# Attention of a hybrid decoder layer: twelve turned chunks per head packed into ten, a third PSUM bank for turning, pair work moved between engines

## The chip, the cores and the metric

One core of one Trainium2 chip runs the whole layer in one launch. The metric is the device time of the launch in microseconds; the kernel before takes 707.17 us in the median of three runs (706.26 to 708.14).

## The reference

Batch 1, 1024 positions, width 1024, all in float32. The layer is a conditioned mixer with two groups of heads that share one input projection:

```python
h = rmsnorm(x, norm_in) * (1.0 + scale) + shift          # shift, scale, gate = silu(c) @ w_ada + b_ada
(cb, cc, cu, cz, aq, ak, av, az, iq, ik, iw) = split(h @ w_in)
y_conv = group_rmsnorm(short_conv_mixer(cb, cc, cu), gn_conv, 8) * silu(cz)
# per query: 8 indexer heads give a score of every key, the 256 best causal keys are kept
score = sum_h iw_h * relu(dot(iq_h, ik) * idx_scale);  sel = top_k(score, 256)
p = softmax(where(selected and causal, q k^T * HEAD_DIM**-0.5, -inf))   # 8 heads of 64
y_attn = group_rmsnorm(p @ v, gn_attn, 8) * silu(az)
out = rmsnorm(x + gate * (concat(y_conv, y_attn) @ w_out), norm_f)   # as the kernel applies it
```

The group norm of the attention divides each head's output by its own root mean square, so the softmax's denominator need not be divided out: it only scales the epsilon. The kernel uses that.

## The kernel before

Every matrix product is made of fp32r products of split operands: a tile X is split into a rounded high part XH (a copy on ScalarE, ACT) and the rest XL (a subtraction on VectorE, DVE, or GpSimd, POOL), and a product is XH·WH + XL·WH + XH·WL. TensorE (PE) therefore does three matmuls where one would do.

The program is written out by hand, one in-order queue for each engine, tied by counting semaphores. It has four stretches: the load and norm of x and the modulation (0 to about 60 us); 37 units of the input projection, between whose matmuls the indexer, the top-k search (on DVE) and the convolution lie (to about 482 us); the attention (482 to 621 us); and the output projection with the last norm (to the end).

The modulation's weights arrive in pieces (`wa`): eight of 512 KB for part 0, and four and four tiles of two 256 KB DMAs for parts 1 and 2. `ada_sum` (L1376 and on) waits with `wa_sem` for its piece, then multiplies and adds on DVE. Each piece of parts 0 and 1 has a semaphore of its own; pairs of pieces of part 2 share one.

The attention handles 8 heads one after the other. For head h the work is:

- `logits(u)`, u = 8h + i: PE makes the logits of query block i (128 queries) against keys 0 to 128(i+1), two matmuls for each 512 columns, into PSUM banks 2-3 (u even) or 0-1 (u odd). `row_max(u)` on DVE adds the mask in place and takes the maximum, `weights(u)` on ACT makes exp into `prob` in SBUF and sums it.
- Turning and values: for each half sb of the queries (blocks 0 to 3, and 4 to 7) and each key block j, a chunk k. `turn(k)` on PE transposes up to four 128x128 tiles of `prob` into a PSUM bank, 4 + k % 2; `split_prob(k)` on ACT copies it out as the high part phH; `low_prob(k)` on DVE subtracts to get phL; `values(k)` on PE multiplies both by V into bank 6 + sb. A head has 12 chunks (STEPS), of 512, 384, 256 and 128 columns in the first half and five of 512, then 384, 256, 128 in the second. `turn(k)` waits for `low_prob(k - 2)`, `values` runs PV_LAG = 2 chunks behind, phH has 3 buffers and phL 2.
- `other_half` (ACT) and `head_out` (DVE) add the two halves of the product and put them in `ya`.

The logits, maxima and exponentials of head h+1 lie between the chunks of head h, at half steps x = 2k, 2k+1 given by the tables LOGITS_AT, MAX_AT and EXP_AT. After every second head there is the work of a pair t (heads 2t, 2t+1) of 128 rows: `square_den` and `keep_den` (DVE) with `denominators` (PE); `pair_square` (POOL, two halves), `group_sums` (PE, one fp32 matmul for each half into banks 3 and 1), `pair_gate` (DVE, 1024 columns) and `pair_add` (DVE, two halves, out of PSUM). For the first three pairs this lies in head 2t+2, so heads 2, 4 and 6 (counted from 0) carry pair work. In heads 2 to 5 ACT and POOL also split one tile of w_out each (`out_high`, `out_low`). In the last head there are no logits to make; 16 steps of the output projection (`out_step`, EARLY_PARTS) lie between the chunks, and ACT and DVE split yconv and w_out. After it `pair_log`, `pair_root` and `pair_scale` finish the attention's gate and norm, and PE goes through the rest of the output projection.

Lines: `turn` L778, `logits` L808 and L809, `values` L890 and L891, `group_sums` L908, `out_step` L939 to L941, `weights` L1142, `split_prob` L1151, `other_half` L1216, `out_high` L1241, `ada_sum` L1378 and L1381, `row_max` L1589, `low_prob` L1597, `head_out` L1605, `pair_gate` L1627, `pair_add` L1636, `pair_scale` L1644, `low_out` L1649, `pair_square` L1818, `out_low` L1823.

## Time and profile before

| what | value |
|---|---|
| median of 3 runs | 707.17 us |
| the profiled execution, its own time | 706.91 us |
| its span, first to last instruction | 704.9 us |
| PE busy | 662.3 us, 94% |
| PE weight loads busy | 546.2 us, 77% |
| DVE busy | 460.4 us, 65% |
| ACT busy | 375.4 us, 53% |
| POOL busy | 207.4 us, 29% |
| mean granted clock of TensorE | 0.997 |

A matmul's busy time is modelled and includes its way through the array, so consecutive matmuls overlap and a PE that is called 90% busy can have more room than 10%. The shares are means over the whole span; the attention has its own, which the rows below show.

### The profile page before, as it was taken

How to read it: one execution, taken by the hardware profiler on the slowest of the kernel's cores; microseconds unless marked ns; L12 is line 12 of the kernel's file. 1: busy time of each engine (PE TensorE's matmuls, PEld its weight loads, DVE VectorE, ACT ScalarE, POOL GpSimd, SP SyncE). 2: the span in 40 equal slices, each digit the busy share in tenths (PEclk: the TensorE clock that was granted, in tenths of full speed). 3: DMA queues.
4: the chain of work that ended last, by engine and by line, in shares of the span. 5: the costliest groups of instructions: out<-in, count | busy, mean ns of one | idle time of the engine just before them, and what ended most of it. 6: DMA issues, size and time to landing. Idle time of an engine off the chain costs nothing.

```text
span 704.9 us, 8934 instructions
## 1 busy us (share of the span) xinstructions
PE 662.3 (94%) x3203; PEld 546.2 (77%) x3203; DVE 460.4 (65%) x777; ACT 375.4 (53%) x558; POOL 207.4 (29%) x105
## 2 busy tenths in 40 slices
PE   0899999899999999999999999999999988999996
PEld 0889977788888888888888887887767666788884
DVE  5894535567889999992079530016898989577635
ACT  5866345556651324453454624636878787784202
POOL 1001223433224334746755667410011110100000
PEclk9999999999999999999999999999999999999999
DMA  8950597533223111111100731085944340221431
GB/s 322 378 203 1 146 156 172 162 96 91 90 89 120 38 53 36 55 60 31 60 32 31 248 110 60 1 179 131 289 120 121 89 121 1 60 91 71 168 120 60
DMA packets 27910, 78.63 MB, mean 112 GB/s; under 512 B 3986, under 2 KB 8410, under 8 KB 27868
## 3 DMA queue, kind: packets, MB, share of 16 engines
q1 hardware_dynamic: 27524, 77.03, 36.8%
q10 hardware_dynamic: 344, 1.05, 0.6%
q8 instruction: 25, 0.41, 0.3%
q14 instruction: 17, 0.14, 0.1%
HBM read 61.25 MB, written 13.41 MB: 106 GB/s over the span
## 4 chain that ended last, share of the span: by engine, by line
PE 72%; DVE 8%; issue 7%; DMA 5%; ACT 4%; SPq 2%; POOL 1%; ACTq 1%; DVEq 0%; POOLq 0%
PE ps L755 15%; PE ps L756 15%; PE ps L757 15%; PE ps L939 4%; PE ps L940 4%; PE ps L941 4%; PE ps L778 3%; DVE acc L1381 2%; DMA raw<-in_w_units 2%; PE ps L828 2%; PE ps L827 2%; PE ps L808 2%; PE ps L809 2%; DMA xin<-in_x 1%; DVE phL L1597 1%
## 5 line engine op out<-in xcount | busy, mean ns | idle before, releaser
L755 PE MATMUL ps<-hH,wH 128*128 128x512 f32 (+1 forms) x544 | 211.8, 389 | 2.0 <-issue 1.9
L757 PE MATMUL ps<-hH,wL 128*128 128x512 f32 (+1 forms) x544 | 210.1, 386 | 0.0
L756 PE MATMUL ps<-hL,wH 128*128 128x512 f32 (+1 forms) x544 | 210.1, 386 | 0.0
L1749 POOL TENSOR_TENSOR wL<-raw,wH 128x1024 fp32r<-128x1024 f32 x35 | 85.4, 2440 | 187.7 <-ACT wH L993 179.5
L755 PEld LDWEIGHTS ps<-hH,wH 128*128 128x128 f32 x544 | 102.2, 188 | 22.5 <-issue 4.0
L757 PEld LDWEIGHTS ps<-hH,wL 128*128 128x128 f32 x544 | 102.1, 188 | 20.4
L756 PEld LDWEIGHTS ps<-hL,wH 128*128 128x128 f32 x544 | 102.2, 188 | 18.3
L1589 DVE CUSTOM_DVE_ANT_0 ps<-ps,bias 128x128 f32<-128x128 f32 (+3 forms) x64 | 48.7, 761 | 45.7 <-PE ps L809 43.7
L1597 DVE TENSOR_TENSOR phL<-ps,phH 128x512 fp32r<-128x512 f32 (+1 forms) x96 | 52.6, 554 | 16.9 <-ACT phH L1151 15.3
L1193 ACT ACTIVATE relu<-ps,wabs 128x384 f32<-128x384 f32 (+5 forms) x48 | 40.1, 849 | 38.1 <-PE ps L828 18.6
L1483 DVE SCALAR_TENSOR_TENSOR score<-relu,wsgn,score 128x384 f32<-128x384 f32 (+5 forms) x42 | 49.7, 1184 | 15.2 <-ACT relu L1193 12.2
L1504 DVE TENSOR_SCALAR_CACHE_REDUCE above<-score,srch 128x384 bf16<-128x384 f32 (+5 forms) x60 | 56.8, 946 | 2.1
L1151 ACT ACTIVATE phH<-ps 128x512 fp32r<-128x512 f32 (+1 forms) x96 | 46.1, 490 | 18.1 <-PE ps L778 16.8
L778 PE MATMUL ps<-identF,prob 128*128 128x128 f32 x288 | 49.1, 280 | 6.8 <-DVE phL L1597 3.6
L1142 ACT ACTIVATE prob<-ps,nmx 128x128 f32<-128x128 f32 (+3 forms) x64 | 47.4, 741 | 15.1 <-DVE nmx L1589 15.1
L778 PEld LDWEIGHTS ps<-identF,prob 128*128 128x128 f32 x288 | 34.5, 141 | 22.9 <-DVE phL L1597 13.1
L940 PE MATMUL ps<-hL,yH 128*128 128x512 f32 x128 | 50.3, 393 | 0.0
L1818 POOL TENSOR_TENSOR ysq<-ya 128x512 f32<-128x512 f32 x8 | 9.9, 1234 | 134.3 <-DVE ya L1605 134.3
L993 ACT ACTIVATE wH<-raw 128x1024 fp32r<-128x1024 f32 x37 | 38.8, 1052 | 10.6 <-DMA raw<-in_w_units 8.3
L890 PE MATMUL ps<-phH,VV 128*128 128x512 f32 (+1 forms) x96 | 38.5, 402 | 0.0
L808 PE MATMUL ps<-ks,qs 128*128 128x512 f32 (+2 forms) x96 | 35.3, 368 | 3.4 <-ACT prob L1142 2.1
L891 PE MATMUL ps<-phL,VV 128*128 128x512 f32 (+1 forms) x96 | 33.1, 346 | 0.0
(225 smaller groups left out, 1129.4 us busy)
## 6 DMA issues: line engine op xcount, KB each, us to landing
raw<-in_w_units SPq DMA_DIRECT2D x36, 512.0 KB, 3.3
ks<-qk_halves SPq DMA_DIRECT2D x32, 256.0 KB, 5.8
xin<-in_x SPq DMA_DIRECT2D x8, 512.0 KB, 7.4
wa<-in_w_ada SPq DMA_DIRECT2D x8, 512.0 KB, 11.8
wa<-in_w_ada SPq DMA_DIRECT2D x16, 256.0 KB, 8.0
gw<-in_w_ada SPq DMA_DIRECT2D x8, 512.0 KB, 4.1
qs<-qk_halves SPq DMA_DIRECT2D x16, 256.0 KB, 4.0
wo<-in_w_out SPq DMA_DIRECT2D x8, 512.0 KB, 9.4
```

The lines of the kernel that those rows point to most:

```text
L755: pe.matmul(out, wH[slot(n)][:, kt, :], hH[:, kt, cols], start=(kt == 0), stop=False)
L756: pe.matmul(out, wH[slot(n)][:, kt, :], hL[:, kt, cols], start=False, stop=False)
L757: mm = pe.matmul(out, wL[slot(n)][:, kt, :], hH[:, kt, cols], start=False, stop=(kt == KT - 1))
L778: mm = pe.transpose(ps[:, 4 + k % 2, P * b:P * b + P], prob_of(sb, b)[:, P * j:P * j + P], identF[:])
L808: pe.matmul(dst[:, o:e], q, ks1[h % 2][:, o:e], start=True, stop=False)
L940: pe.matmul(out, yH[b % 4][:, ct, :], hL[:, ct, cols], start=False, stop=False)
L1142: A(prob_of(sb, i % 4), logit_bank(u), ACT.Exp, bias=nmx[:, u:u + 1], scale=-1.0, accum_out=den[:, h // 2, h % 2, i:i + 1]).then_inc(s_exp, 1)
L1483: v.scalar_tensor_tensor(score_of(i), relu[:, u % 2, 0:n], wsgn[:, i, h:h + 1], score_of(i), ALU.mult, ALU.add).then_inc(s_score, 1)
L1504: v.tensor_scalar(above[:, 0:(i + 1) * P], score_of(i), cand[:, b:b + 1], None, ALU.is_ge, ALU.add, accum_out=count[:, b:b + 1]).then_inc( ...
L1589: v.tensor_tensor_reduce(src, src, bias_of(i), -ATT_SCALE, 3.0e38, ALU.add, ALU.min, nmx[:, u:u + 1]).then_inc(s_mx, 1)
L1597: v.tensor_tensor(phL[:, k % 2, P * c:HALF], ps[:, 4 + k % 2, P * c:HALF], phH[:, k % NPH, P * c:HALF].bitcast(F32), ALU.subtract).then_in ...
L1749: g.tensor_tensor(wL[slot(n)][:], raw[slot(n)][:], wH[slot(n)][:].bitcast(F32), ALU.subtract).then_inc(s_wL, 1)
```

## The change

A head has ten chunks in place of twelve. CHUNKS lists the key blocks of each: blocks 1 and 3 of the first half share a bank (384 and 128 columns), as do blocks 5 and 7 of the second. A packed bank is split by one instruction of 512 columns on ACT and one on DVE; `turn` and `values` handle the two blocks one after the other. The transposes and the matmuls stay the same in number and width.

Turning uses three banks in rotation: 4, 5, and a third that is borrowed, the upper half of a logits pair (3, or 0 in the last head) or the first half's output bank (6), by the step in the head. `turn(k)` waits for `low_prob(k - 3)`, and for the borrowed bank to be free; `values` runs three chunks behind, phH has 4 buffers and phL 3. To make room in SBUF `ysq` has one buffer in place of two. The tables of the half steps are new.

For the first three pairs, `pair_gate` and `pair_add` go from DVE to POOL, each in two halves. POOL does not read the sums in PSUM, so ACT copies each half out first (`keep_sums`). The group sums of both halves use bank 1. The multiplication by gn_attn goes from the gate to `pair_scale`, which becomes a scalar_tensor_tensor. The last pair stays on DVE.

Of the modulation's weights, pieces 0 and 1 of part 0 share a semaphore, as do 2 and 3, and of part 1 pieces 0 and 1, and 2 and 3 (WA_SHARES). A wait on such a semaphore is for both pieces. New semaphores are s_ygP, s_addP and s_sums.

```diff
+WA_SHARES = ((0, 0, 1, 1, 2, 3, 4, 5), (0, 0, 1, 1), (0, 0, 1, 1))
...
-NPH = 3
-PV_LAG = 2
-STEPS = 12
-LOGITS_AT = (4, 11, 13, 16, 18, 21, 23, 26)
-MAX_AT = (6, 11, 14, 16, 17, 22, 23, 25)
-EXP_AT = (10, 14, 17, 17, 22, 24, 27, 30)
+NPH = 4
+NPL = 3
+PV_LAG = 3
+CHUNKS = ([(0,)] + [(1, 3)] + [(2,)], [(j,) for j in range(5)] + [(5, 7)] + [(6,)])
+STEPS = len(CHUNKS[0]) + len(CHUNKS[1])
+LOGITS_AT = (2, 5, 10, 13, 15, 16, 18, 20)
+MAX_AT = (1, 5, 9, 12, 14, 15, 17, 20)
...
-TMP_AT, OUT_AT = 4, 5
+TMP_AT, OUT_AT = 5, 5
+THIRD_IN_OUT = (7, 8, 9, 0, 1)
...
-SUMS_AT = {24 * (2 * t + 2) + 11 + 4 * half: (t, half) for t in range(NT - 1) for half in range(2)}
-SUMS_AT[LAST + 17] = (NT - 1, 0)
-GATE_AT = {24 * (2 * t + 2) + 12: t for t in range(NT - 1)}
-ADD_AT = {24 * (2 * t + 2) + 13 + 4 * half: (t, half) for t in range(NT - 1) for half in range(2)}
-ADD_AT[LAST + 16] = (NT - 1, 0)
...
+HEAD = 2 * STEPS
...
+SUMS_AT = {HEAD * (2 * t + 2) + 5 + 8 * half: (t, half) for t in range(NT - 1) for half in range(2)}
+SUMS_AT[LAST + 15] = (NT - 1, 0)
+KEEP_SUMS_AT = {HEAD * (2 * t + 2) + 6 + 8 * half: (t, half) for t in range(NT - 1) for half in range(2)}
+OUT_HIGH_AT = {HEAD * (2 + ct) + 13: ct for ct in range(4)}
+OUT_HIGH_AT.update({LAST + x: 4 + n for n, x in enumerate((11, 14, 17, 18))})
+OUT_LOW_AT = {LAST + x: 4 + n for n, x in enumerate((13, 18, 19))}
+EARLY_PARTS = {3: 2, 4: 2, 5: 2, 6: 2, 7: 3, 8: 3, 9: 2}
...
                 [at(f"prob1_{b}", [P, (b + 5) * P], F32, kb) for b, kb in enumerate((186, 65.5, 68.5, 72))]]
         phH = at("phH", [P, NPH, HALF], F32R, 80)
-        phL = at("phL", [P, 2, HALF], F32R, 88)
+        phL = [at(f"phL{i}", [P, HALF], F32R, kb) for i, kb in enumerate((88, 90, 78))]
...
         woB = [at(f"woB{i}", [P, 2, D], F32R, kb) for i, kb in enumerate((145, 113))]
-        ysq = [at(f"ysq{i}", [P, HALF], F32, kb) for i, kb in enumerate((86, 205))]
+        ysq = at("ysq", [P, HALF], F32, 205)
...
+        CH = [(h, sb, js) for h in range(NH) for sb in range(2) for js in CHUNKS[sb]]
+        CH_AT = {(h, sb, j): n for n, (h, sb, js) in enumerate(CH) for j in js}
...
+        def all_up_to(h, sb, j):
+            return max(CH_AT[(h, sb, x)] for x in range(j + 1))
         def last_chunk(g):
-            return CH_AT[(g // 2, g % 2, 4 * (g % 2) + 3)]
+            return all_up_to(g // 2, g % 2, 4 * (g % 2) + 3)
...
+            return range(max(0, j - 4 * sb), 4)
+        def place(js, sb, j):
+            return -P * blocks_of(sb, j).start if js.index(j) else 0
+        def width(k):
+            h, sb, js = CH[k]
+            return slice(0 if len(js) > 1 else P * blocks_of(sb, js[0]).start, HALF)
...
-            return (1, 7)[half]
+            return 7 if t == NT - 1 and half else 1
+        def turn_bank(k):
+            h, at_step = k // STEPS, k % STEPS
+            if k % 3 < 2:
+                return 4 + k % 3
+            if at_step in THIRD_IN_OUT:
+                return 6
+            return 3 if h < NH - 1 else 0
+        def turned_into(bank, h, steps):
+            ks = [STEPS * h + x for x in steps if turn_bank(STEPS * h + x) == bank]
+            return ks[-1] + 1 if ks else 0
...
-            return s_wa[g][i // 2] if g == 2 else s_wa[g][i]
+            return s_wa[g][WA_SHARES[g][i]]
...
-                h, sb, j, c = CH[k]
-                if j == 0:
+                h, sb, js = CH[k]
+                bank, at_step = turn_bank(k), k % STEPS
+                if js[0] == 0:
                     pe.wait_ge(s_exp, NB * h + 4 * sb + 4 if k else 6)
-                if k >= 2:
-                    pe.wait_ge(s_pl, k - 1)
-                for b in range(c, 4):
-                    mm = pe.transpose(ps[:, 4 + k % 2, P * b:P * b + P], prob_of(sb, b)[:, P * j:P * j + P], identF[:])
+                if k >= 3:
+                    pe.wait_ge(s_pl, k - 2)
+                if bank == 6:
+                    pe.wait_ge(s_o, 2 * h + 1 if at_step > 5 else 2 * h - 1)
+                elif bank == 3:
+                    pe.wait_ge(s_exp, NB * h + (7 if h else 8))
+                elif bank == 0:
+                    pe.wait_ge(s_exp, NB * NH)
+                for j in js:
+                    for b in blocks_of(sb, j):
+                        o = P * b + place(js, sb, j)
+                        mm = pe.transpose(ps[:, bank, o:o + P], prob_of(sb, b)[:, P * j:P * j + P], identF[:])
                 mm.then_inc(s_tp, 1)
...
+                if h >= 3 and h % 2 == 1 and i == 5:
+                    pe.wait_ge(s_sums, h - 1)
+                if h and i == 4:
+                    pe.wait_ge(s_pl, turned_into(3, h - 1, range(2, 7)))
...
-                h, sb, j, c = CH[k]
+                h, sb, js = CH[k]
...
-                if j == 0 and g >= 2:
+                if js[0] == 0 and g >= 2:
                     pe.wait_ge(s_o, g - 1)
-                out = ps[:, 6 + sb, P * c:HALF]
-                pe.matmul(out, VV[:, j, h, :], phH[:, k % NPH, P * c:HALF], start=(j == 0), stop=False, skip_group_check=True)
-                pe.matmul(out, VV[:, j, h, :], phL[:, k % 2, P * c:HALF], start=False, stop=(j == 4 * sb + 3),
-                          skip_group_check=True).then_inc(s_pv, 1)
+                if k % STEPS == 0 and turned_into(6, h, (0, 1)):
+                    pe.wait_ge(s_pl, turned_into(6, h, (0, 1)))
+                for j in js:
+                    cols = slice(P * blocks_of(sb, j).start, HALF)
+                    src = slice(cols.start + place(js, sb, j), cols.stop + place(js, sb, j))
+                    out = ps[:, 6 + sb, cols]
+                    pe.matmul(out, VV[:, j, h, :], phH[:, k % NPH, src], start=(j == 0), stop=False, skip_group_check=True)
+                    mm = pe.matmul(out, VV[:, j, h, :], phL[k % NPL][:, src], start=False, stop=(k == last_chunk(g)),
+                                   skip_group_check=True)
+                mm.then_inc(s_pv, 1)
...
-                    pe.wait_ge(s_exp, NB * (2 * t + 2) + 7 + half)
+                    pe.wait_ge(s_exp, NB * (2 * t + 2) + 8)
+                    if half:
+                        pe.wait_ge(s_sums, 2 * t + 1)
...
-                pe.matmul(ps[:, sums_bank(t, half), :], pairs[:], ysq[half][:], start=True, stop=True).then_inc(s_yss, 1)
+                pe.matmul(ps[:, sums_bank(t, half), :], pairs[:], ysq[:], start=True, stop=True).then_inc(s_yss, 1)
...
+                        pe.wait_ge(s_pl, turned_into(0, NH - 1, range(2, 7)))
                         if half:
-                            pe.wait_ge(s_add, 2 * NT - 1)
+                            pe.wait_ge(s_add, 1)
...
+            def keep_sums(t, half):
+                act.wait_ge(s_yss, 2 * t + half + 1)
+                act.wait_ge(s_ygP, 2 * t + half + 1)
+                A(pair_cols(t, half), ps[:, sums_bank(t, half), :], ACT.Copy).then_inc(s_sums, 1)
             def pair_log(t, half=None):
-                act.wait_ge(s_add, 2 * t + (half if half is not None else 1) + 1)
+                if t < NT - 1:
+                    act.wait_ge(s_addP, 2 * t + 2)
+                else:
+                    act.wait_ge(s_add, half + 1)
                 z = pair_cols(t, half)
...
-                dve.wait_ge(wa_sem(g, i), 16 * each * (2 if g == 2 else 1))
+                dve.wait_ge(wa_sem(g, i), 16 * each * WA_SHARES[g].count(WA_SHARES[g][i]))
...
-                if k >= 2:
-                    dve.wait_ge(s_pv, k - 1)
-                v.tensor_tensor(phL[:, k % 2, P * c:HALF], ps[:, 4 + k % 2, P * c:HALF],
-                                phH[:, k % NPH, P * c:HALF].bitcast(F32), ALU.subtract).then_inc(s_pl, 1)
+                if k >= NPL:
+                    dve.wait_ge(s_pv, k - NPL + 1)
+                v.tensor_tensor(phL[k % NPL][:, width(k)], ps[:, turn_bank(k), width(k)],
+                                phH[:, k % NPH, width(k)].bitcast(F32), ALU.subtract).then_inc(s_pl, 1)
...
+            def pair_scale(t):
+                dve.wait_ge(s_yrs, t + 1)
+                dve.wait_ge(s_ygP, 2 * t + 2)
+                v.scalar_tensor_tensor(ya[:, t, :], ya[:, t, :], vec[:, V_GA + t:V_GA + t + 1], azs[:, t, :],
+                                       ALU.mult, ALU.mult).then_inc(s_ya, 1)
...
+                if t or half:
+                    pool.wait_ge(s_yss, 2 * t + half)
                 z = ya[:, t, HALF * half:HALF * half + HALF]
-                g.tensor_tensor(ysq[half][:], z, z, ALU.mult).then_inc(s_ysq, 1)
...
+            def pair_gate(t, half):
+                pool.wait_ge(s_ysq, 2 * t + half + 1)
+                cols = slice(HALF * half, HALF * half + HALF)
+                g.tensor_tensor(ya[:, t, cols], ya[:, t, cols], azs[:, t, cols], ALU.mult).then_inc(s_ygP, 1)
+            def pair_add(t, half):
+                pool.wait_ge(s_sums, 2 * t + half + 1)
+                pool.wait_ge(s_din, 32 * (t + 1))
+                cols = slice(HALF * half, HALF * half + HALF)
+                g.tensor_tensor(azs[:, t, cols], azs[:, t, cols], dden[:, cols], ALU.add).then_inc(s_addP, 1)
+            for t in range(NT - 1):
+                pair_square(t, 0)
+                pair_gate(t, 0)
+                if t:
+                    out_low(2 * t - 1)
+                pair_square(t, 1)
+                pair_gate(t, 1)
+                pair_add(t, 0)
+                pair_add(t, 1)
+                if t < 2:
+                    out_low(2 * t)
             pair_square(NT - 1, 0)
```

## Rows read from the trace of the kernel before

**Rows 1.** PE's busy time: stretch, length, busy (count), clock, DMA share, GB/s

```profile
100.00:420.00 320.00, 316.12 (x1429) 1.00 0.30 90
...
660.00:705.00 45.00, 38.20 (x169) 0.98 0.26 94
```

**Rows 2.** Busy time by head: stretch, length, PE, PEld, DVE, ACT, POOL, clock, DMA

```profile
514.27:531.46 17.19, 15.91 (x90) 11.88 (x88) 15.65 (x34) 13.50 (x32) 3.45 (x2) 1.00 0.41 95
531.46:547.19 15.73, 14.09 (x87) 11.33 (x85) 13.77 (x33) 13.37 (x32) 3.38 (x2) 1.00 0.54 136
...
580.08:598.00 17.92, 16.59 (x92) 12.18 (x90) 16.40 (x34) 13.27 (x33) 1.04 (x1) 1.00 0.01 1
...
598.80:620.88 22.08, 21.20 (x100) 16.61 (x101) 13.46 (x22) 18.46 (x27) 2.08 (x1) 0.92 0.16 49
```

**Rows 3.** Groups by form, DVE, 514.27 to 547.19: busy us, mean ns, idle before

```profile
L1597 DVE TENSOR_TENSOR phL<-ps,phH 128x512 fp32r<-128x512 f32 x12 | 8.2, 687 | 2.2 <-ACT phH L1151 1.9
L1589 DVE CUSTOM_DVE_ANT_0 ps<-ps,bias 128x1024 f32<-128x1024 f32 x3 | 3.7, 1233 | 0.3
...
L1597 DVE TENSOR_TENSOR phL<-ps,phH 128x384 fp32r<-128x384 f32 x4 | 2.2, 552 | 0.0
...
L1636 DVE TENSOR_TENSOR azs<-ps,dden 128x512 f32<-128x512 f32 x2 | 1.4, 680 | 0.0
L1627 DVE SCALAR_TENSOR_TENSOR ya<-ya,vec,azs 128x1024 f32<-128x1024 f32 x1 | 1.3, 1280 | 0.0
...
L1597 DVE TENSOR_TENSOR phL<-ps,phH 128x128 fp32r<-128x128 f32 x4 | 1.1, 287 | 0.0
```

**Rows 4.** Groups by form, ACT, the same stretch

```profile
L1151 ACT ACTIVATE phH<-ps 128x512 fp32r<-128x512 f32 x12 | 7.1, 596 | 2.5 <-PE ps L778 2.5
...
L1216 ACT ACTIVATE tmp<-ps 64x512 f32<-64x512 f32 x4 | 2.4, 592 | 0.1
L1142 ACT ACTIVATE prob<-ps,nmx 128x1024 f32<-128x1024 f32 x2 | 2.2, 1110 | 0.0
...
L1151 ACT ACTIVATE phH<-ps 128x384 fp32r<-128x384 f32 x4 | 1.9, 487 | 0.0
...
L1151 ACT ACTIVATE phH<-ps 128x128 fp32r<-128x128 f32 x4 | 1.1, 278 | 0.9 <-PE ps L778 0.8
```

**Rows 5.** Waits, same stretch: who for whom, us in total, times, longest

```profile
PE ps L778 <- ACT prob L1142: 0.6, 2, 0.3
...
ACT phH L1151 <- PE ps L778: 3.4, 9, 0.8
...
DVE phL L1597 <- ACT phH L1151: 1.9, 4, 0.9
```

**Rows 6.** Order of time: start us, us, instruction [idle before]; POOL and DVE

```profile
549.96 1.04 POOL L1818 TENSOR_TENSOR ysq<-ya 128x512 f32<-128x512 f32 x1 [7.54 <-DVE ya L1605]
...
610.62 2.08 POOL L1818 TENSOR_TENSOR ysq<-ya 128x512 f32<-128x512 f32 x1 [26.72 <-DVE ya L1605]
...
610.57 1.23 DVE L1649 TENSOR_TENSOR hL<-wo,woB 128x1024 fp32r<-128x1024 f32 x1
```

**Rows 7.** Order of time, ACT and DVE, 534 to 536 us

```profile
534.69 0.60 ACT L1151 ACTIVATE phH<-ps 128x512 fp32r<-128x512 f32 x1 [0.58 <-PE ps L778]
...
535.32 0.69 DVE L1597 TENSOR_TENSOR phL<-ps,phH 128x512 fp32r<-128x512 f32 x1 [0.89 <-ACT phH L1151]
```

**Rows 8.** DVE's sums of part 0, and the issues of pieces 2 and 3

```profile
21.43 8.24 DVE L1381 SCALAR_TENSOR_TENSOR acc<-wa,small,acc 128x1024 f32<-128x1024 f32 x6
...
L524 SPq DMA_DIRECT2D wa<-in_w_ada x2: 480/1245/2010, 7.8 to 8.3; - x2
DMA to landing us min/median/max: 12.6/13.0/13.4
```

**Rows 9.** The last head: PE's time and granted clock in one microsecond; order of time

```profile
602.00:603.00 1.00, 1.00 (x4) 0.50 0.01 4
...
601.26 0.77 PE L939 MATMUL ps<-hH,yH 128*128 128x512 f32 x1 [0.45 <-issue]
```

More of the change, by code:

```diff
@@ L1145, in split_prob @@
             def split_prob(k):
-                h, sb, j, c = CH[k]
                 act.wait_ge(s_tp, k + 1)
@@ L1262, in _ @@
                         other_half(TMPS[x])
+                    if x in KEEP_SUMS_AT:
+                        keep_sums(*KEEP_SUMS_AT[x])
                     if x in OUT_HIGH_AT:
@@ L1694, in _ @@
                 low_y(b, 1)
-            pair_scale(NT - 1, 1)
+            last_scale(1)
             dve.wait_ge(s_gate, 16)
```

112 lines of the change are left out of this document (45 added, 67 removed).

## The prediction

> **What bounds the kernel now.** I read the whole kernel first by stretches, then the attention head by head. In the middle of the projection PE is busy 316.12 of 320 us [rows 1]; nothing in the change touches PE's work there, so it stays. Of the 45 us from 660 on PE is busy for the first 38.2, to its last matmul at 698.2 [rows 1], and what follows is the last block's norm; that stays too. So only the attention can move, and what it gains or loses moves the end one for one, as long as PE then has the output projection's operands in time.
>
> In the attention the windows by head [rows 2] show two kinds of head. Head 3 (1 and 5 are the same within 0.02) lasts 15.73 us with DVE 13.77, ACT 13.37 and PE 14.09 busy; heads 2 and 6 (4 is as 2), which carry the pair work, last 17.19 and 17.92 with DVE 15.65 and 16.40 busy, ACT still 13.5 and 13.3. DVE grows by 1.88 from one kind to the other and the head by 1.46. PE's number is modelled, and the head follows DVE, not PE, so I take DVE as the nearest limit, ACT next, and PE as the one that waits. No engine is full, however: in a light head DVE has 1.96 us idle. The largest piece is one wait of 0.89 at the head's start [rows 7]: ACT has ended the last exponential and stands 0.58 us until PE has turned the next chunk, and DVE, behind ACT, starts only at 535.32. With two banks PE can't turn that chunk ahead. Over two heads ACT waits 3.4 us in nine places for turns, DVE 1.9 for splits [rows 5]. So a head costs DVE's work plus about 10% in round trips over the two banks.
>
> **Packing.** Per head two chunks go. On DVE a 384 and a 128 instruction (552 + 287 ns) become one of 512 (687): 0.15 us by durations, twice, 0.30 [rows 3]; busy times overlap a little back to back, so I take 0.2. On ACT 487 + 278 - 596 = 0.17, twice, 0.34 [rows 4]; I take 0.3. On PE two waits go and no work.
>
> **Pair work, heads 2, 4, 6.** DVE loses one gate of 1.28 and two adds of 0.68, 2.64 us by durations [rows 3]; the difference of DVE's busy time between the two kinds of head (1.88, where the light ones have about 0.45 of denominator work instead) says 2.3 to 2.4, which I take. ACT gains two copies of 512 columns out of PSUM at the 0.59 of the tmp copy [rows 4]: +1.2. The trace doesn't show a wait for `keep_sums`: it stands early in the head behind the last exponential, PE's sum and the gate on POOL. Behind it in ACT's queue are the next split and so DVE's next chunk. I bound its wait by 0 and by 0.9 (the longest of DVE's waits [rows 5]) and take 0.3. POOL gains two gates and two adds at 1.04 each [rows 6], 4.2 us a pair, beside the 3.4 that it does in a head now [rows 2]: some 11 us in the 33 us of two heads. Its half 1 chain (square and gate, 2.1 us after `head_out` at half step 5) has until half step 14, four and a half chunks, some 6 us: hidden. If each ran at the 2.08 of the disturbed square it would still take 4.2.
>
> This last case is one for the Trainium skill. At 610.62 POOL's square took 2.08 us in place of 1.04 while DVE ran a subtraction with both inputs in SBUF, itself not slowed (1.23) [rows 6]. The page "GPSIMD Engine Reference", section "Specifications", says that POOL shares its SBUF interfaces with DVE and contends with DVE instructions that have two SBUF inputs, and its section on engine selection gives elementwise work to VectorE; it speaks against the move. By its rule the price falls where DVE's inputs are both in SBUF; here `low_prob`, `head_out` and `row_max` all read PSUM, and the sum stays.
>
> **The new limits.** Light head: DVE 13.77 - 0.2 = 13.6, ACT 13.37 - 0.3 = 13.1. Pair head: DVE 15.65 - 0.2 - 2.35 = 13.1, ACT 13.5 - 0.3 + 1.2 = 14.4. So the limit of the pair heads moves from DVE to ACT.
>
> **Three banks, lag 3.** A chunk's round trip is a turn (some 0.6, by the 0.58 that ACT stood for one [rows 7]), a split of 0.60 and a subtraction of 0.69, with the handing over some 2.1 us. Over two banks that is 1.05 us a chunk at best, over three 0.7, where the queues need 1.36 to 1.5 a chunk. So a turn can nearly always be made ahead, and most of DVE's 1.96 us of idle time in a light head should go, of which the waits for splits, 0.95 a head by the mean of two, are the half. Not all: the first chunk of a head's second half still needs the eighth exponential (the PE wait of 0.3, twice, in [rows 5]), logits for a new head need the seventh, and a borrowed bank has waits of its own: bank 3 on that same seventh exponential, which lies one step ahead on ACT, and bank 6 on `head_out`, also a step ahead. I bound the gain from this between 0 and 1.4 in a head (1.96 less what 33 hand-overs of some 20 ns cost). For a light head I take 0.9, the size of the wait that the extra bank answers to [rows 7]; with the 0.2 of DVE the head goes from 15.73 to 14.6, a gain of 1.1. For a pair head: 14.4 of ACT work, 0.3 for `keep_sums`, and the 0.9 to 1.0 us that a head still loses at its start and in handing over, 15.7; from 17.19 that is 1.5.
>
> **The last head.** It lasts 22.08 us, ACT busy 18.5, PE 21.2. Its mean granted clock is 0.92: for about 3.5 us around 602 it was 0.50, the lower level (1.2 GHz), and 8% of the head, 1.8 us, were lost [rows 2, 9]; at 601.26 PE had just stood 0.45 us. If PE waits less there, the fall may not come: a gain of 1.8. Against that, ten steps leave less time: PE's group sum at half step 15 needs POOL's square after `head_out` at half step 11, and the second half of block 1 needs the add; PE could stand 1 us. Range of the term -2.2 to +1.0; I take -0.7.
>
> The page "TensorE: Matmul & The Clock Gate" of the Trainium skill, section "A second HAM failure mode: psum-queue depth-cycling", says that a PE that idles a little between groups as banks cycle can swing between the clocks. By that the term would be near -2.
>
> **Weights' semaphores.** DVE makes seven sums of part 0, the last six from 21.43 to 29.67 without a gap, 1.39 us apart [rows 8]; the sum of piece 2, at 22.83, now also needs piece 3. That was issued at 8.3 and landed 13.4 later, at 21.7: 1.1 us of cover. Piece 1, issued ahead of piece 2 in one queue, should be in ahead of it, and piece 2 is by 20.4 (7.8 and 12.6), before the second sum. Cost nothing; without the cover, each microsecond of lateness of piece 3 costs one, since these sums lie on the chain. Part 1's sums come 8 us after part 0's, and its DMAs follow on in the same queue; nothing. **`pair_scale`** becomes a form that took 1.28 us as the gate [rows 3] in place of one of some 1.2, three times, 0.2 us after the attention, behind it PE has 48 matmuls of blocks 2 and 3 queued: nothing. One `ysq` buffer: the square of half 1 comes later than the sum of half 0 in any case: nothing.
>
> **The sum.** Heads 0, 1, 3, 5: 4 x 1.1 = 4.4. Heads 2, 4, 6: 3 x 1.5 = 4.5. Last head 0.7. Together 9.6, from the profiled execution's own 706.91 (its span of 704.9 and 2.0 around it): 697.3 us. The median of the runs is 0.26 above that execution, within their spread, so I leave it.
>
> **Rivals.**
> (a) The banks give all: every named wait goes, light heads at 14.2 (1.5 saved), pair heads at ACT's 14.4 plus 0.4 (2.4), last head 2.0. 6.0 + 7.2 + 2.0 = 15.2, 691.7 us. For it: a turn can be three chunks ahead, and the waits are of the kind that this removes. Against: each queue stays in order and the two exponentials at the head's border are still in series.
> (b) The waits only change their names: the tables' order, not the banks, makes them. Then light heads gain the 0.3 of packing and pair heads 0.7 (DVE's relief less ACT's load). 1.2 + 2.1 = 3.3, 703.6 us. For it: DVE waited only four times in two heads for a split.
> (c) Slower: the eighth exponential. `turn` of the second half waits for it on PE, and behind it there are the values and the logits of the next head. Before, it had its place after the third split of a head, now after the second; its own chain is a maximum of 1.23 and an exponential of 1.11 [rows 3, 4], with their logits and reads of the sums some 3.6 us. If it comes later than the three steps give, some 4.1 us, PE, then ACT and DVE stand. It decides from 1.3 us of extra wait a head: by then light heads (4 x 1.1) and pair heads (3 x 1.5) have nothing left; at 2.0 light heads lose 0.9 and pair heads 0.5 each and the last head gains nothing: 3.6 + 1.5 = 5.1, 712.0 us. Against: the maximum of that block is already behind turn 0 and the chain fits by half a microsecond.
>
> **How the numbers follow.** Forecast 0.57, (a) 0.22, (b) 0.13, (c) 0.08. About 0.3% (2.1 us) is what a measurement of this kernel can tell from no change. Faster by more than that means under 705.0: all of the forecast and of (a), most of (b), 0.87 together, cut to 0.85 for what the unknown wait of `keep_sums` could add. Same 0.07, slower 0.08. The range: at the bottom into (a), 690; at the top (b) with a little more, 704.5.
>
> **What would show it.** Light heads near 14.6 us and pair heads near 15.7 in the windows; DVE's wait for splits at a head's start under 0.3; DVE about 13.1 busy in a pair head and ACT 14.4, ACT now first; POOL's gates and adds at about 1.04. The start of PE's projection unchanged, at the same microsecond. The clock in the last head tells its term. Wrong it would be if PE's waits for exponentials grow past a microsecond a head, if ACT stands before the copy of the sums, or if the heads stay at their length while the idle time moves from DVE to another.

## The result, and the profile after

The changed kernel takes 698.49 us (median of six runs, 696.65 to 699.95), the kernel before 706.71 beside it; the ratio is 0.9881, 95% interval 0.9857 to 0.9906. The forecast was 697.3. The profiled execution took 698.44 us with a span of 696.6: 8.3 less than before.

The attention again head by head, now from the start of one head's last exponential (1024 columns) to the start of the next. Cut in this way heads 0 to 6 of before last 16.77, 15.72, 17.18, 15.73, 17.18, 15.72 and 17.18 us. The windows of the kernel after; columns: stretch, length, PE busy (count), PEld, DVE, ACT, POOL, granted clock, DMA share, GB/s; the answer to [rows 2]:

```profile
483.44:499.83 16.39, 14.85 (x83) 12.72 (x83) 12.22 (x28) 12.76 (x29) 0.00 (x0) 0.90 0.92 299
499.83:514.31 14.48, 13.68 (x87) 11.52 (x86) 13.37 (x31) 12.32 (x29) 2.33 (x2) 1.00 0.79 212
514.31:529.86 15.55, 15.16 (x90) 12.15 (x89) 12.93 (x29) 14.24 (x32) 7.21 (x5) 1.00 0.45 102
529.86:543.97 14.11, 13.69 (x87) 11.64 (x86) 13.29 (x31) 13.16 (x30) 4.68 (x3) 1.00 0.60 151
543.97:559.48 15.51, 15.14 (x90) 12.26 (x89) 12.88 (x29) 14.25 (x32) 7.23 (x5) 1.00 0.43 103
559.48:574.55 15.07, 13.75 (x87) 11.54 (x86) 13.38 (x31) 13.16 (x30) 4.67 (x3) 1.00 0.57 138
574.55:590.07 15.52, 15.08 (x93) 12.36 (x91) 12.94 (x29) 13.41 (x31) 4.86 (x4) 1.00 0.01 2
```

Read down the lengths first. The seven heads gave 8.85 us. The three light heads 1, 3 and 5 gained 1.24, 1.62 and 0.65, though the same work is done in each; the pair heads gained 1.63, 1.67 and 1.66. In a pair head DVE fell from 15.65 to 12.9 and ACT rose from 13.5 to 14.2. In head 3 PE is busy 13.69 of 14.11 us, where before it was 14.09 of 15.73.

The groups by form of DVE and then ACT over heads 2 and 3 (columns as in [rows 3, 4], to which they answer), and below them POOL in order of time in head 2 (start, us, instruction, idle before), against [rows 6]:

```profile
L1653 DVE TENSOR_TENSOR phL<-ps,phH 128x512 fp32r<-128x512 f32 x17 | 11.7, 687 | 1.1 <-ACT phH L1197 1.1
L1653 DVE TENSOR_TENSOR phL<-ps,phH 128x256 fp32r<-128x256 f32 x4 | 1.7, 422 | 0.4 <-ACT phH L1197 0.3
...
L1197 ACT ACTIVATE phH<-ps 128x512 fp32r<-128x512 f32 x17 | 10.2, 597 | 1.5 <-PE ps L814 1.4
...
L1272 ACT ACTIVATE azs<-ps 128x512 f32<-128x512 f32 x2 | 1.2, 600 | 0.1
```

```profile
517.44 1.04 POOL L1880 TENSOR_TENSOR ysq<-ya 128x512 f32<-128x512 f32 x1 [8.77 <-DVE ya L1661]
518.56 1.28 POOL L1891 TENSOR_TENSOR ya<-ya,azs 128x512 f32<-128x512 f32 x1
519.80 1.30 POOL L1898 TENSOR_TENSOR azs<-azs,dden 128x512 f32<-128x512 f32 x1
523.86 1.29 POOL L1898 TENSOR_TENSOR azs<-azs,dden 128x512 f32<-128x512 f32 x1 [2.76 <-ACT azs L1272]
```

The durations on DVE and ACT are those of before. POOL's gate and add take 1.28 to 1.30 us each, not the 1.04 of its square, but POOL stood 2.76 us before one of them, so it has room. ACT hardly stands before `keep_sums` (0.1).

Over the same two heads the waits, against [rows 5], columns: who for whom, us in total, times, longest:

```profile
DVE ps L1646 <- PE ps L847: 1.9, 3, 1.1
...
ACT phH L1197 <- PE ps L814: 1.4, 6, 0.2
DVE phL L1653 <- ACT phH L1197: 1.4, 4, 0.7
...
PE ps L846 <- ACT prob L1189: 0.4, 1, 0.4
PE ps L846 <- DVE phL L1653: 0.4, 1, 0.4
```

ACT's waits for turns fell from 3.4 us to 1.4, and no single one is above 0.2. DVE now waits for logits instead, that is, for PE: 1.9 us where it was 0.5. What is left of PE's own waits is 0.8 in two heads.

Outside these heads two things moved, and together they give back 0.62. DVE's sums of the weights are not one of them: they still follow one another in 1.39 us without a gap, so the shared semaphores cost nothing, as [rows 8] had it:

```profile
22.45 8.24 DVE L1438 SCALAR_TENSOR_TENSOR acc<-wa,small,acc 128x1024 f32<-128x1024 f32 x6
```

(They begin 1.02 us later than before, but so does DVE's whole queue: its first square of x starts at 13.45 instead of 12.47, when x has landed.) The attention starts 0.37 us later than before. In the kernels whose edits touch nothing ahead of it this start varies from 482.6 to 484.1, and is 484.9 to 485.3 in E7, E9 and E11, in whose profiles the granted clock fell once near 130 us; so I read nothing into it. And from the last head's exponential to the end of PE's last matmul it is 99.90 us after 99.65: nothing gained, which hides terms of opposite sign (below, with the step "last head").

### The profile page after: what moved, and what is told of

It reads as the page before. It is cut to its first block, busy times and chain, and to the rows that moved or that the text cites. A ratio compares the mean times of both kernels' runs of the same rounds, so it can differ in the third digit from the quotient of the medians.

```text
span 696.6 us, 8911 instructions
## 1 busy us (share of the span) xinstructions
PE 658.8 (95%) x3203; PEld 548.5 (79%) x3203; DVE 450.7 (65%) x752; ACT 376.7 (54%) x548; POOL 222.3 (32%) x117
## 3 DMA queue, kind: packets, MB, share of 16 engines
q10 hardware_dynamic: 344, 1.05, 0.6%
## 4 chain that ended last, share of the span: by engine, by line
PE 77%; DVE 7%; DMA 5%; ACT 4%; issue 3%; SPq 2%; POOL 1%; ACTq 1%; DVEq 0%
PE ps L782 15%; PE ps L783 15%; PE ps L784 15%; PE ps L986 4%; PE ps L987 4%; PE ps L988 4%; PE ps L814 3%; PE ps L846 3%; DVE acc L1438 2%; PE ps L847 2%; DMA raw<-in_w_units 2%; PE ps L866 2%; PE ps L865 2%; PE ps L934 2%; PE ps L933 2%
## 5 line engine op out<-in xcount | busy, mean ns | idle before, releaser
L1653 DVE TENSOR_TENSOR phL<-ps,phH 128x512 fp32r<-128x512 f32 (+1 forms) x80 | 50.5, 634 | 14.4 <-ACT phH L1197 11.3
L1197 ACT ACTIVATE phH<-ps 128x512 fp32r<-128x512 f32 (+1 forms) x80 | 44.1, 552 | 9.1 <-PE ps L814 8.6
L814 PE MATMUL ps<-identF,prob 128*128 128x128 f32 x288 | 45.7, 278 | 1.1 <-ACT prob L1189 0.8
L933 PE MATMUL ps<-phH,VV 128*128 128x512 f32 (+1 forms) x96 | 36.8, 384 | 0.0
```

The costliest lines, as they stand in the source:

```text
L814: mm = pe.transpose(ps[:, bank, o:o + P], prob_of(sb, b)[:, P * j:P * j + P], identF[:])
L933: pe.matmul(out, VV[:, j, h, :], phH[:, k % NPH, src], start=(j == 0), stop=False, skip_group_check=True)
L1653: v.tensor_tensor(phL[k % NPL][:, width(k)], ps[:, turn_bank(k), width(k)], phH[:, k % NPH, width(k)].bitcast(F32), ALU.subtract).then_inc ...
```

## The experiments

The length of a head is the measure that tells most here: the total also carries the start and short falls of the granted clock, which come at other places from one execution to the next. The table has every kernel's seven heads, from its one profiled execution, and its time; "before" for each call lay between 706.7 and 707.7. Head 0 holds a fall of the clock in the kernel after, E2, E4 and E7, heads 1, 3 and 5 each hold one in E5, and none of the other heads in the table does.

| kernel | head 0 | 1 | 2 | 3 | 4 | 5 | 6 | median us | ratio to before (interval) |
|---|---|---|---|---|---|---|---|---|---|
| before | 16.77 | 15.72 | 17.18 | 15.73 | 17.18 | 15.72 | 17.18 | 706.71 | |
| after | 16.39 | 14.48 | 15.55 | 14.11 | 15.51 | 15.07 | 15.52 | 698.49 | 0.9881 (0.9857-0.9906) |
| E1 two banks | 15.27 | 14.52 | 15.77 | 14.53 | 16.01 | 14.51 | 15.77 | 699.54 | 0.9898 (0.9873-0.9922) |
| E2 pair work on DVE | 16.40 | 14.48 | 17.24 | 14.11 | 16.60 | 15.05 | 16.60 | 702.57 | 0.9928 (0.9906-0.9950) |
| E3 both | 15.29 | 14.52 | 17.00 | 14.52 | 16.99 | 14.51 | 17.05 | 703.64 | 0.9952 (0.9934-0.9970) |
| E4 step 6 in the out bank | 16.41 | 14.50 | 17.43 | 14.13 | 15.52 | 15.83 | 15.53 | 700.91 | 0.9924 (0.9895-0.9953) |
| E5 before, lag 3 | 18.35 | 18.54 | 18.93 | 18.56 | 18.92 | 18.55 | 18.18 | 720.49 | 1.0195 (1.0173-1.0218) |
| E6 after, PE loaded | 15.73 | 15.16 | 16.46 | 14.86 | 16.44 | 15.78 | 16.46 | 705.73 | 0.9986 (0.9955-1.0017) |
| E7 after, DVE loaded | 16.61 | 14.86 | 16.13 | 14.87 | 15.52 | 15.81 | 15.52 | 702.65 | 0.9935 (0.9915-0.9956) |
| E8 after, ACT loaded | 15.09 | 14.73 | 15.76 | 14.55 | 15.72 | 15.30 | 15.55 | 700.61 | 0.9902 (0.9878-0.9927) |
| E9 E3 with lag 2 | 15.60 | 14.67 | 17.23 | 14.68 | 17.23 | 14.68 | 17.26 | 705.62 | 0.9973 (0.9956-0.9989) |
| E10 before, PE loaded | 17.40 | 16.34 | 17.83 | 16.35 | 17.82 | 16.33 | 17.82 | 712.86 | 1.0068 (1.0042-1.0095) |
| E11 before, DVE loaded | 17.77 | 16.77 | 17.99 | 16.77 | 17.99 | 16.78 | 18.00 | 712.38 | 1.0068 (1.0043-1.0093) |
| E12 bank at fixed steps | 14.81 | 14.12 | 15.51 | 14.11 | 15.51 | 14.10 | 15.54 | 696.47 | 0.9855 (0.9826-0.9884) |

**E1: the changed kernel with two banks.**

```diff
-            if k % 3 < 2:
-                return 4 + k % 3
-            if at_step in THIRD_IN_OUT:
-                return 6
-            return 3 if h < NH - 1 else 0
+            return 4 + k % 2
...
-                if k >= 3: pe.wait_ge(s_pl, k - 2)
+                if k >= 2: pe.wait_ge(s_pl, k - 1)
```

> The kernel after with turning over banks 4 and 5 only (turn k waits for the subtraction of k-2); packing, lag 3, tables, pair work on POOL stay. Theory A (round trips over two banks were the main cost, the third bank removed them): heads without pair work go from 14.1-14.5 back to about 15.4 us, pair heads from 15.5 to about 16.8, in all +8 us, about 706. Rival B (the relief of DVE by packing and by moving the pair work did it, the third bank is beside the point): under 0.3 us a head, in all under +2 us, about 700.

Heads 1 to 6 sum to 91.11 us against 90.24 with three banks. (All seven sum to 106.38 against 106.63, but head 0 of the kernel after has a fall of the clock in it.) Heads 2, 3, 4 and 6 are 0.22 to 0.50 longer without the third bank, but head 5 is 0.56 shorter. The theory that the round trip over the banks was the main cause, with 8 us in all, fell.

**E2: the changed kernel, gates and adds of the pairs back on DVE** (and no `keep_sums`).

```diff
-            def pair_gate(t, half):  # POOL; pair_add likewise
-                g.tensor_tensor(ya[:, t, cols], ya[:, t, cols], azs[:, t, cols], ALU.mult)
+            def pair_gate(t, half):  # DVE; pair_add reads ps directly
+                v.tensor_tensor(ya[:, t, cols], ya[:, t, cols], azs[:, t, cols], ALU.mult)
```

> The kernel after with gate and add of the first three pairs back on DVE (in halves of 512 columns, out of PSUM), no copy of the sums on ACT, none of it on POOL; three banks and packing stay. Theory A: heads without pair work unchanged (14.1 to 14.5), pair heads get 2.4 us of DVE work on 12.9 and with three banks DVE can run nearly full: about 16.3 us for 15.5, in all +2.4 us, about 701. Rival B: pair heads back to 17.2, in all +5 us, about 703.5.

The light heads stay to 0.02 us; the pair heads lose 1.69, 1.09 and 1.08. That lies between the two expectations in heads 4 and 6, and head 2 is at the rival's 17.2.

**E3: both of these**, so packing, lag 3 and the new tables, with the small changes that cost nothing or were not tested by themselves: the shared semaphores, one `ysq` buffer, and the pair work in halves.

> Both undone: two banks and pair work on DVE; of the change only the packing, lag 3, the new tables and the weights' semaphores are left. Theory A: the same as the kernel before within 2 us (packing gives about 0.3 us a head, the new tables are made for three banks and may cost as much), 704 to 707. Rival B: packing gives what the light heads gained (1.3 to 1.6 us a head), so about 701.

Here 1.2 us of each light head is already gained, with two banks, and 0.1 to 0.2 of each pair head. The time, 703.64, lies just under A's range; the light heads gained nearly what B says. From E3 to E1 only the pair work moves: its heads gain 1.23, 0.98 and 1.28 and the light ones nothing.

**E4: in the changed kernel, a third chunk of step 6 goes to bank 6** rather than 3 (heads 2 and 5).

```diff
-THIRD_IN_OUT = (7, 8, 9, 0, 1)
+THIRD_IN_OUT = (6, 7, 8, 9, 0, 1)
```

> The kernel after with step 6 of a head turning into bank 6 in place of bank 3 (only heads 2 and 5 have their third bank there). In the trace after, PE stands 0.91 us in head 5 at the logits of block 4 for the subtraction of step 6, which still holds bank 3, and the head lasts 15.07 where head 3 lasts 14.11. Theory: that wait goes, head 5 about 14.3, head 2 unchanged at 15.5 (or 0.2 longer, the turn now waits for head_out one step earlier); in all -0.8 us. Rival: the wait for head_out in bank 6 takes its place and head 5 stays at 15.0.

Both accounts missed: head 5 grew by 0.76 and head 2 by 1.88. PE in order of time in head 2 (start, us, instruction, idle before and its releaser):

```profile
521.04 0.63 PE L814 MATMUL ps<-identF,prob 128*128 128x128 f32 x4 [1.71 <-DVE ya L1661]
```

PE stands 1.71 us until `head_out` has let the out bank go. A borrowed bank has an owner, and its release is a new wait; in the changed kernel itself the same step, in bank 3, holds up the logits of head 5, and 0.91 of the 0.96 us that head 5 is longer than head 3 is here:

```profile
567.44 0.47 PE L846 MATMUL ps<-ks,qs 128*128 128x512 f32 x1 [0.91 <-DVE phL L1653]
```

**E5: the kernel before with lag 3** (its buffers, and one `ysq` buffer in place of two).

```diff
-NPH = 3
-PV_LAG = 2
+NPH = 4
+PV_LAG = 3
...
-                if k >= 2: dve.wait_ge(s_pv, k - 1)
+                if k >= 3: dve.wait_ge(s_pv, k - 2)
```

> The kernel before with only the values three chunks behind instead of two (four buffers of the rounded weights, three of the remainders), and one buffer of squares instead of two; nine chunks a head, two banks and the old tables stay. Theory (the lag takes the round trip that PE waited for in every head): heads 1, 3 and 5 fall from 15.72 to about 14.5 us, the 14.52 that the packing with the lag gave in the kernel with two banks and the pair work on DVE. Rival (the ten chunks and the new tables with them): those heads stay within 0.3 us of 15.72. In heads 2, 4 and 6 the second square now waits for the first one's sum, so they are not a clean measure: 17.0 to 17.6. Total by the theory about 703.5, by the rival 706 to 708.

(The kernel before has twelve chunks a head; "nine", here and in the expectation of E9, is a slip of mine.) Both accounts missed. The light heads grew by 2.8 us, heads 2 and 4 by 1.7, head 6 by 1.0. But each of the light heads holds a fall of the granted clock, which the pair heads do not. Heads 2 and 3:

```profile
519.49:538.42 18.93, 15.78 (x90) 11.85 (x88) 15.79 (x33) 13.53 (x32) 3.42 (x2) 1.00 0.35 84
538.42:556.98 18.56, 15.53 (x87) 12.80 (x85) 13.82 (x32) 13.48 (x33) 3.39 (x2) 0.91 0.45 112
```

At a mean clock of 0.91 that is some 1.7 of the 2.8 (0.09 of 18.56, an estimate), so the lag itself costs a light head about 1.1. ACT in order of time in head 2:

```profile
524.18 0.59 ACT L1216 ACTIVATE tmp<-ps 64x512 f32<-64x512 f32 x1 [1.31 <-PE ps L891]
...
537.52 0.59 ACT L1216 ACTIVATE tmp<-ps 64x512 f32<-64x512 f32 x1 [0.81 <-PE ps L891]
```

ACT copies the finished group out at a fixed place of its queue. With the values one chunk later that place is too early: ACT stands 1.31 and 0.81 us before these copies, 4.4 us over heads 2 and 3, where the kernel before has no such wait that the profile names; its waits for turns fell only from 3.4 to 2.7. Lag and tables go together.

**E9: E3 with the lag back at 2** (and the buffers of before, phH 3 and phL 2).

```diff
-PV_LAG = 3
+PV_LAG = 2
```

> The kernel of the packing alone (ten chunks, two banks, the pair work on DVE, the new tables) with the values two chunks behind instead of three and the buffers of before. It did light heads in 14.52 us against 15.72 before. Theory (packing and lag work together: the nine chunks with lag 3 grew to 18.55 because ACT stood at its copy of the finished group, so neither is good alone): light heads at 15.2 to 15.8, the time at 706 to 708. Rival (the packing with its tables gives the gain alone and the lag is idle): light heads within 0.3 of 14.52, the time at 703 to 704.5.

The rival held in the heads; the time, 705.62, is above its 703 to 704.5. Light heads 14.67: packing with its tables gives 1.05 of the 1.2 by itself, the lag 0.15. Pair heads stay as before (17.23 against 17.18), and the lag gives 0.2. That packing is worth nothing there is not shown, for E9's pair heads also have one `ysq` buffer and the pair work in halves, and what these cost was not measured. A light head of each, before and E9:

```profile
532.74:548.47 15.73, 14.09 (x86) 11.33 (x85) 13.77 (x33) 13.37 (x33) 3.38 (x2) 1.00 0.53 132
```

```profile
532.41:547.09 14.68, 13.84 (x86) 11.45 (x85) 13.40 (x31) 13.26 (x31) 3.43 (x2) 1.00 0.61 145
```

DVE's work fell by 0.37 and ACT's by 0.11; PE without work fell from 1.64 to 0.84. So most of the 1.05 is standing time, not instructions. The wait of 0.89 at the head's start, which the prediction put down to the two banks [rows 7], is gone here with two banks and lag 2, as it is in the kernel after. DVE in head 3 of E9, then of the kernel after:

```profile
535.52 1.43 DVE L1639 TENSOR_TENSOR phL<-ps,phH 128x512 fp32r<-128x512 f32 x2 [0.24 <-ACT phH L1191]
```

```profile
532.96 1.36 DVE L1653 TENSOR_TENSOR phL<-ps,phH 128x512 fp32r<-128x512 f32 x2 [0.23 <-ACT phH L1197]
```

Whether the two fewer chunks take the time or the new places in the tables was not separated: the tables' steps are counted in chunks, so the one does not run without the other.

**E6, E7, E8: the changed kernel with more work on one engine in every head.** What they compute in addition is read by nothing.

```diff
+                    if e - o == HALF and o == 0:          # E6, logits, five a head
+                        pe.matmul(dst[:, o:e], q, ks1[h % 2][:, o:e], start=True, stop=True)
```

```diff
+                if k % STEPS in (0, 3, 6) and k >= FIRST_TURNS:   # E7 on DVE; E8 a Copy of the same on ACT
+                    v.tensor_tensor(scratch[:], ps[:, turn_bank(k), P:HALF],
+                                    phH[:, k % NPH, P:HALF].bitcast(F32), ALU.subtract)
```

> The changed kernel with five more matmuls a head of 512 columns (the first half of the logits of blocks 3 to 7 is computed once more, nothing reads it), some 5 x 0.23 = 1.15 us more of PE a head. Theory (after the change PE itself is the limit of a head, 97% busy): heads 1 to 6 grow by 1.0 to 1.2 us each and the time by about 7.5 to 8, to 706 to 707. Rival (ACT is the limit, as the prediction had it, and PE waits for it): heads grow by less than 0.6 us, the time by 2 to 4.

> The changed kernel with three more subtractions of 384 columns a head on DVE (after those of steps 0, 3 and 6, into an unused buffer), some 3 x 0.48 = 1.4 us more of DVE a head. Theory (PE is the limit): DVE has about 1.1 to 2.2 us to spare in a head (13.3 busy of 14.1 to 15.5), so the heads grow by 0.2 to 0.8 us, less than half of the load. Rival (DVE, or the round trip through it, is the limit): 1.2 us and more a head.

> The changed kernel with three more copies of 384 columns a head on ACT (at steps 0, 3 and 6, into an unused buffer), some 3 x 0.42 = 1.2 us more of ACT a head. Theory (PE is the limit): ACT has 1 us to spare (13.2 of 14.1 in a light head, 14.24 of 15.55 in a pair head), so the heads grow by under 0.6 us. Rival (ACT is the limit, as the prediction had it for heads 2, 4 and 6): those three heads grow by 1.0 to 1.3 us, the others by less.

Heads 2 and 3 of E6, then of E7, then of E8:

```profile
520.29:536.75 16.46, 15.92 (x96) 13.11 (x94) 13.06 (x29) 14.27 (x32) 7.22 (x5) 1.00 0.41 97
536.75:551.61 14.86, 14.32 (x93) 12.53 (x91) 13.42 (x31) 13.19 (x31) 4.69 (x3) 1.00 0.61 143
```

```profile
516.48:532.61 16.13, 15.32 (x90) 12.15 (x89) 14.05 (x32) 14.27 (x33) 7.23 (x5) 1.00 0.42 98
532.61:547.48 14.87, 13.72 (x87) 11.61 (x86) 14.35 (x34) 13.28 (x30) 4.66 (x3) 1.00 0.58 142
```

```profile
512.43:528.19 15.76, 15.19 (x90) 12.14 (x90) 12.87 (x29) 15.11 (x35) 7.23 (x5) 1.00 0.54 131
528.19:542.74 14.55, 13.94 (x88) 11.61 (x87) 13.07 (x31) 14.00 (x34) 4.67 (x3) 1.00 0.59 145
```

(The load on DVE and ACT stands ahead of the chunk's own subtraction or split, not behind it as the expectation of E7 has it.)

PE's load made heads 1 to 6 longer by 0.68 to 0.94, mean 0.82. Its busy time grew by 0.63 to 0.84, but that is modelled and can hide short stands; by their spacing of 0.23 us the five matmuls are 1.15, so some 0.7 of each microsecond came through. The expectation of 1.0 to 1.2 was missed from below. DVE's load (1.0 to 1.2 of busy time) cost 0.38, 0.76 and 0.74 in the light heads, and 0.58, 0.01 and 0 in heads 2, 4 and 6. ACT's (0.8 to 0.9) cost 0.23 in the mean, and in the pair heads, where I had taken ACT for the limit, 0.21, 0.21 and 0.03. So in pair heads PE is the nearest limit, and ACT is not, though it is busy 14.24 of 15.55. In light heads the load on DVE, which is the larger, cost about as much as that on PE: neither is shown to be the limit there alone.

**E10, E11: the same loads in the kernel before** (E11 at steps 0, 4 and 7).

> The kernel before with the same five extra matmuls of 512 columns a head (about 0.8 us more of PE's busy time, as in the changed kernel, where a light head grew by 0.7 and a pair head by 0.93 us). Theory (before, PE had about 2 us a head in which it waited, so it wasn't the limit): heads 1, 3 and 5 grow by 0 to 0.4 us from 15.72, heads 2, 4 and 6 by 0 to 0.4 from 17.18; the time by 0 to 3. Rival (PE was as much the limit before, since its own work stands in the round trip): 0.7 to 0.9 us a head, 5 to 6 in all.

> The kernel before with three more subtractions of 384 columns a head on DVE (1.0 to 1.1 us more of busy time; after the change they cost 0.4 us a head). Theory (before, DVE and the round trip through it set the heads, most of all 2, 4 and 6, where it is 15.64 busy of 17.18): pair heads grow by 0.9 to 1.4 us, light heads by 0.6 to 1.2; the time by 5 to 8. Rival (DVE has as much to spare as after the change): 0.4 us a head, 3 in all.

Head 3 of E10, then of E11:

```profile
539.57:555.92 16.35, 15.06 (x91) 12.21 (x90) 13.55 (x33) 13.51 (x32) 3.38 (x2) 1.00 0.56 131
```

```profile
537.84:554.61 16.77, 14.05 (x86) 11.36 (x85) 14.86 (x36) 13.47 (x32) 3.38 (x2) 1.00 0.52 125
```

DVE's 1.1 us cost a light head 1.05 and a pair head 0.81; after the change it is 0.63 and 0.20 in the mean. PE's load cost 0.63 for 0.9 of busy time (1.15 by the spacing), nearer to the rival than to my theory of 0 to 0.4: PE's work stood in the round trip of before as well, although PE waited. (In E6 and E10 the attention also starts 5 to 6 us later than in the kernels they load, 1.2 of it for the five matmuls in head 0's own logits by their spacing of 0.23 us; about 1.6 by the estimate below is a fall of the clock near 132 us in both; the rest I can't put down to the edit, so their totals aren't used.)

**E12: the third bank at steps 2, 5 and 8 of every head but the last**, in place of every third chunk, which wanders to steps 1, 4, 7 (heads 1, 4) and 0, 3, 6, 9 (heads 2, 5).

```diff
+THIRD_AT = {h: (2, 5, 8) if h < NH - 1 else (1, 4, 7) for h in range(NH)}
-            if k % 3 < 2:
-                return 4 + k % 3
+            if at_step not in THIRD_AT[h]:
+                return 4 + (k - sum(x % STEPS in THIRD_AT[x // STEPS] for x in range(k))) % 2
-                if k >= 3:
-                    pe.wait_ge(s_pl, k - 2)
+                same = [x for x in range(k) if turn_bank(x) == bank]
+                if same:
+                    pe.wait_ge(s_pl, same[-1] + 1)
```

> The changed kernel with the third bank at steps 2, 5 and 8 of every head but the last, as heads 0, 3 and 6 have it, instead of wandering (steps 1, 4, 7 in heads 1 and 4; 0, 3, 6, 9 in heads 2 and 5); the other chunks take the two banks in turn, and each turning waits for the last one in its own bank. Theory (head 5 at 15.07 and head 1 at 14.48 against 14.11 in head 3 are only the place of the third bank): heads 1 and 5 fall to 14.1 to 14.2, heads 2, 4 and 6 stay at 15.5; the time falls by 1.3 us, to about 697. Rival (the place of the third bank doesn't matter, head 3 owes its 14.11 to its place between pair heads): heads as in the changed kernel within 0.2 us, the same time.

```profile
497.99:512.11 14.12, 13.73 (x87) 11.64 (x86) 13.29 (x31) 12.34 (x30) 2.32 (x2) 1.00 0.79 228
...
557.24:571.34 14.10, 13.69 (x87) 11.63 (x86) 13.29 (x31) 13.17 (x30) 4.69 (x3) 1.00 0.61 148
```

Heads 1 and 5 came to 14.12 and 14.10, as the theory had it; heads 1 to 6 together are 1.35 us shorter than in the changed kernel. The median is 2.0 lower, but the two intervals (0.9826-0.9884 and 0.9857-0.9906) overlap: that it beats the changed kernel is shown by its heads, not by its time. Against E1 the third bank is now worth 0.40, 0.42 and 0.41 in light heads and 0.26, 0.50 and 0.23 in pair heads.

## Why the prediction was right in its sum and wrong in its steps

| term | forecast | measured | what made it |
|---|---|---|---|
| light heads 1, 3, 5 | 3 x 1.1 | 1.24, 1.62, 0.65 | packing and tables 1.05, lag 0.15, bank -0.56 to 0.42 |
| head 0 | 1.1 | 0.38 | a fall of the clock took some 1.6; to be read with the last head |
| pair heads 2, 4, 6 | 3 x 1.5 | 1.63, 1.67, 1.66 | move to POOL 1.0 to 1.3, lag 0.2, bank 0.22 to 0.50, packing and the work in halves together 0 |
| last head | 0.7 | -0.25 | new stands and work moved into this stretch, against the clock's fall of before |
| weights' semaphores, `pair_scale`, `ysq` | 0 | 0 | as forecast |
| start of the attention | 0 | -0.37 | not explained |
| together | 9.6 | 8.2 | |

**Right.** The size of a pair head (15.7 forecast, 15.5 measured), DVE's relief (13.1 forecast, 12.9), ACT's load (14.4, 14.2), the cover of the weight sums, DVE's wait for a split at a light head's start (under 0.3, 0.23; in head 2 it is still 0.71) and the mean light head (14.6, 14.55). ACT's wait for `keep_sums` was priced at 0.3 and is 0.1 in two heads. That POOL hides the pair work held: its gates and adds took a quarter more than forecast and nobody waited for them. DVE's subtractions stayed at 687 ns beside them, as the sum assumed. The Trainium skill's page "GPSIMD Engine Reference", section "Specifications", warns of contention with DVE instructions that have two SBUF inputs; these subtractions have one input in PSUM, and the trace shows none.

**The step "Three banks, lag 3" failed.** It gave a light head 0.9 us from the bank and the lag and 0.2 from the packing. E9, E3 and E1 have it the other way round: 1.05 from packing with its tables, 0.15 from the lag, and in the changed kernel the bank gives heads 1, 3 and 5 together -0.1; at its best steps (E12) it gives 0.4 a head, so bank and lag never reached the 0.9. The named wait that this 0.9 was read from goes with two banks too (E9). I priced the packing by the time of its instructions alone. But each chunk is also a hand-over PE to ACT to DVE to PE; I had the round trip's 2.1 us in the text and didn't count two fewer of them. Packing's price by that account, two chunks at some 0.5 each, would have been near. That PE's time without work fell by 0.8 fits; that the hand-overs made it, and not the new places in the tables, is argued, not shown.

**The step "limit of the pair heads moves to ACT" failed.** The sum of ACT's busy time and a margin came out at the right length by luck: E8 shows that ACT's 0.9 us more hardly moves them, E6 that PE's does. [rows 2] had PE at 15.91 in a pair head, above the 14.4 of ACT; I set it aside because PE's busy time is modelled. After the change head 3 is PE's 13.7 plus 0.4.

**The step "last head" was mis-sized, inside its bounds.** It took 1.8 us for a fall of the clock that would not come, less 1.1 for new stands. The fall did not come, but nothing was gained. E10 does in this stretch what the kernel before does, and had no fall: 98.13 us to the end of PE's last matmul, where before took 99.65 and after takes 99.90. So without the clock the stretch grew by 1.8. PE's idle time explains 0.74 of that (1.88 us after, 1.14 in E10). The other 1.0 is busy time. What fits it is that the stretch begins at the last exponential, which now has another place among PE's work (the last entry of EXP_AT is 23 with heads of 20 half steps, 30 with heads of 24 before, and the values run a chunk later). Head 0's window has lost at least as much: PE is busy 13.3 to 13.7 us in it in E12, E1 and E3, 15.11 before, while in a light head it fell by only 0.2 to 0.4. So head 0 and the last head are one term, forecast as 1.8 and measured as 0.13 with one fall on each side; without falls, by E12's head 0 and E10, it is 0.19. That the sum of all terms still came out near is luck in part: light and pair heads gave 0.7 more than forecast.

The waits of PE from 590 us on in the changed kernel; before, three stands of 0.9, 0.5 and 0.3 were in their place:

```profile
PE ps L814 <- ACT prob L1189: 0.8, 1, 0.8
PE ps L941 <- DVE dsq L1668: 0.6, 1, 0.6
PE ps L986 <- DVE yL L1718: 0.4, 1, 0.4
PE ps L986 <- DVE azs L1693: 0.2, 1, 0.2
```

Two sums of the prediction don't come out: 33 hand-overs of 20 ns from 1.96 leave 1.3, not 1.4, and rival (b)'s 0.7 for a pair head should be DVE's 2.35 less ACT's 1.2, some 1.15, which puts (b) near 702.3. Rival (a) was held back by the last head and by the bank's wandering. (b) was half right: not the banks but the tables and the packing made the light heads' gain, which it put at 0.3 and which was 1.2 in the mean. (c) didn't come: in heads 2 and 3 PE's matmuls wait 0.4 us for exponentials, and its weight loads 1.8, where it was 1.2.

## What to carry to other kernels

Price a step of a pipeline by its hand-overs too, not only by its instructions: where three engines pass chunks round, two fewer chunks of twelve, with the tables that go with them, gave a microsecond a head with the same columns. Before you name a limit, load each engine a little and see whose microsecond comes through; an engine that is busy 92% of a head can have slack (ACT here), and one that "only waits" can pass most of a load on. Cut two kernels for comparison at marks that have the same place in the work, or work that moves across the mark looks like a gain and a loss. A third buffer borrowed from another use should be taken at the same, chosen steps in every round: wandering every third chunk, it gave with one head what it took in another.
